# Delta-rule head of a hybrid decoder layer: ScalarE reads, a table load, mask and layer-norm steps put into other slots

## The reference, cut to what matters

```python
proj = rmsnorm(x, g_pre_mix) @ w_in   # q, k, v | beta, decay | z | GLU input | gate a | gate b
qkv  = silu(causal_dwconv(qkv_pre, conv_qkv_w))          # width 4
q, k = l2norm(q) * HEAD_K ** -0.5, l2norm(k)
...
a    = where(strict, beta * (k @ k.T) * exp(gam_i - gam_j), 0)   # chunks of 64 positions
sol  = triangular_solve(a + eye, [beta * v, beta * exp(gam) * k])
...
o    = rmsnorm(o) * silu(z)
glu  = glu_in[..., :CONF_WIDTH] * sigmoid(glu_in[..., CONF_WIDTH:])
c    = causal_dwconv(glu, conf_dw_w) + conf_dw_b         # width 31
o_b  = silu(layernorm(c, conf_ln_g, conf_ln_b))
x    = x + rmsnorm((sigmoid(gate_a) * o + sigmoid(gate_b) * o_b) @ w_out)
y    = x + rmsnorm(square(relu(rmsnorm(x) @ w_up)) @ w_down)
```

## Time and profile before

| | us |
|---|---|
| time, median of 3 runs | 1051.16 (1051.08 to 1052.3) |
| the profiled execution | 1051.12 |
| its span | 1049.3 |
| TensorE busy | 1031.2 (98%), 7929 products |
| VectorE busy | 739.0 (70%) |
| GpSimd busy | 647.9 (62%) |
| ScalarE busy | 595.3 (57%) |
| granted TensorE clock | 0.9 or more of full speed in every slice |

### The profile page before, as it was taken

One profiled execution on the slowest core, in us unless ns is written; L12 is line 12 of the kernel. 1 busy time (PEld: TensorE's weight loads), 2 busy tenths in 40 slices (PEclk: granted clock), 3 DMA queues, 4 the chain that ended last, 5 costly groups with the idle time before them and its releaser, 6 DMA issues.

```text
span 1049.3 us, 21800 instructions
## 1 busy us (share of the span) xinstructions
PE 1031.2 (98%) x7929; PEld 1001.8 (95%) x7929; DVE 739.0 (70%) x1240; ACT 595.3 (57%) x1100; POOL 647.9 (62%) x568
## 2 busy tenths in 40 slices
PE   8999999999999999999999999999999999999997
PEld 6999899999999999999999999999999999999997
DVE  7989898898888988889767757594444444444335
ACT  7865646575565655656747855765444343343632
POOL 1895777785877858677684433647555555555631
PEclk9999999999999999999999999999999999999999
DMA  6322312223132231323221162123322233222302
GB/s 240 114 70 82 108 42 92 95 80 104 43 95 93 96 90 40 94 93 111 96 79 43 54 241 82 41 81 101 101 81 82 81 94 107 80 80 80 119 6 88
DMA packets 33883, 94.36 MB, mean 90 GB/s; under 512 B 4864, under 2 KB 12576, under 8 KB 33824
## 3 DMA queue, kind: packets, MB, share of 16 engines
q1 hardware_dynamic: 33824, 93.57, 27.3%
HBM read 85.02 MB, written 8.53 MB: 89 GB/s over the span
## 4 chain that ended last, share of the span: by engine, by line
PE 81%; DVE 6%; issue 4%; POOL 3%; ACT 3%; DVEq 0%; ACTq 0%; POOLq 0%
PE ps L784 26%; PE ps L1214 15%; PE ps L1162 13%; PE ps L793 7%; PE ps L1246 5%; PE ps L749 3%; DVE ps L1964 2%; DVE t_r L1961 1%; PE ps L936 1%; POOL in_lo L2659 1%; DVE work L2195 1%; PE ps L803 1%; POOL o_a L2659 1%; DVE work L2092 1%; POOL work L2659 1%
## 5 line engine op out<-in xcount | busy, mean ns | idle before, releaser
L2659 POOL TENSOR_TENSOR w_lo<-raw,w_hi 128x1024 fp32r<-128x1024 f32 x100 | 240.8, 2409 | 149.5 <-ACT w_hi L1790 50.2
L784 PE MATMUL ps<-in_hi,w_hi 128*128 128x288 f32 x944 | 285.9, 303 | 1.2 <-ACT work L1447 0.7
L784 PE MATMUL ps<-in_lo,w_hi 128*128 128x288 f32 x944 | 281.8, 300 | 0.7 <-POOL in_lo L2659 0.7
L784 PE MATMUL ps<-in_hi,w_lo 128*128 128x288 f32 x944 | 282.0, 299 | 0.0
L1964 DVE SCALAR_TENSOR_TENSOR ps<-work,ct,ps 128x512 f32<-128x512 f32 x240 | 180.7, 753 | 7.9 <-DVE work L2124 1.6
L784 PEld LDWEIGHTS ps<-in_hi,w_hi 128*128 128x128 f32 x944 | 177.6, 188 | 3.9 <-issue 2.4
L784 PEld LDWEIGHTS ps<-in_hi,w_lo 128*128 128x128 f32 x944 | 177.6, 188 | 0.7 <-issue 0.2
L784 PEld LDWEIGHTS ps<-in_lo,w_hi 128*128 128x128 f32 x944 | 177.2, 188 | 1.0 <-POOL in_lo L2659 0.9
L1961 DVE TENSOR_TENSOR o_a<-o_a,ps 128x576 f32<-128x576 f32 (+1 forms) x63 | 42.8, 682 | 107.6 <-PE ps L1214 73.3
L2659 POOL TENSOR_TENSOR w_lo<-t_pair,w_hi 128x1024 fp32r<-128x1024 f32 x18 | 43.6, 2423 | 42.5 <-ACT w_hi L1819 29.7
L2659 POOL TENSOR_TENSOR work<-work 128x576 f32<-128x576 f32 (+4 forms) x51 | 57.9, 1148 | 15.1 <-PE ps L1049 10.8
(11 more groups left out here) (408 smaller groups left out, 2816.7 us busy)
## 6 DMA issues: line engine op xcount, KB each, us to landing
raw<-w_all_in SPq DMA_DIRECT2D x135, 512.0 KB, 3.7
work<-s_in_in SPq DMA_DIRECT2D x8, 512.0 KB, 3.3
s_sample_out<-work SPq DMA_DIRECT2D x8, 512.0 KB, 4.4
xt<-x_t_in SPq DMA_DIRECT2D x4, 576.0 KB, 6.6
xt<-x_t_in SPq DMA_DIRECT2D x2, 1152.0 KB, 7.2
work<-decay_rows SPq DMA_DIRECT2D x7, 288.0 KB
y_out<-o_a SPq DMA_DIRECT2D x14, 144.0 KB, 1.8
halo<-halos_in SPq DMA_DIRECT2D x9, 156.0 KB, 3.6
```

The costliest lines, as they stand in the source:

```text
L784: t = mm(dense_ps(n, j, h), a[:, w, k], b[:, k, h * HALF:(h + 1) * HALF], start=r == 0, stop=r == PASS_MM // 2 - 1)
L2659: return gp.tensor_tensor(out, a, b, op)
```

## The change

It moves steps between slots. No step of the computation is added or left out but for the pieces into which `um` is cut.

1. TensorE: `MIDDLE_AT` of slots 19 and 20 goes from 11, 8 to 10, 9.
2. ScalarE, passes 1 to 7: the read of CB's first half (slot 18) goes behind the copies to `x_r` and `u_r`; the sigmoid table is loaded in slot 16, behind the casts. In every pass, slot 19 begins with a copy of one quarter of `t_r` into `um`.
3. GpSimd: the rest of `um` is formed in slot 16, after level 6, in two smaller subtractions; `tmi_ready` now counts two a pass.
4. VectorE: the fourth tap of V's convolution goes from slot 19 to slot 20, behind `x_last`; pass 3's table `early_3` changes.
5. Pass 1: the channel sum goes behind `chunk_u` within slot 24.
6. Last pass: the exponentials go from slot 2 to slot 3, with that behind the read of Z's second half and a cast; from slot 17 on layer norm's subtractions and pairs go behind `head(n, s)`; the last pair and the three sums go from slot 19 to slot 20, where they stand behind `x_last`; the squares of slot 18 go behind the `x_r` and `u_r` copies.

```diff
-MIDDLE_AT = (12, 12, 14, 14, 14, 14, 12, 13, 12, 10, 10, 12, 10, 13, 11, 13, 12, 11, 11, 11, 8, 8,
+MIDDLE_AT = (12, 12, 14, 14, 14, 14, 12, 13, 12, 10, 10, 12, 10, 13, 11, 13, 12, 11, 11, 10, 9, 8,
              10, 12, 8, 10, 4, 12, 4, 4, 15, 0)
...
+            def channel_sum(n):
+                act.wait_ge(conv31_done, n)
...
             def phase(n):
-                for s in range(33):
+                def mean_squares(s):
+                    for k in (2 * s - 30, 2 * s - 29):
+                        act.wait_ge(xc_ready, k + 1)
+                        A(xc_squares(k), conf[:, k], ACT.Square).then_inc(xc_sq, 1)
+
+                def read_first(s):
                     pos, j = evac_first(n, s)
...
+                for s in range(33):
+                    if s == 19:
+                        act.wait_ge(t_ready, LEVELS * n)
+                        A(quad(v["um"], 1, 0), quad(t_r, 1, 0).bitcast(F32), ACT.Copy).then_inc(tmi_ready, 1)
+                    if last(n) or s != 18:
+                        read_first(s)
                     pos, j = evac(n, s)
...
                     casts(n, s)
+                    if not last(n) and s == 16:
+                        act.preload_act_table_set("sigmoid_and_others")
...
-                    if s == (11 if last(n) else 24 if n_is(n, 1) else 19):
...
+                    if not n_is(n, 1) and s == (11 if last(n) else 19):
+                        channel_sum(n)
...
-                    if last(n) and 15 <= s < 19:
-
-                        for k in (2 * s - 30, 2 * s - 29):
-                            act.wait_ge(xc_ready, k + 1)
-                            A(xc_squares(k), conf[:, k], ACT.Square).then_inc(xc_sq, 1)
+                    if last(n) and 15 <= s < 18:
+                        mean_squares(s)
...
-                    if s == (3 if n_is(n, 1) else 2):
+                    if s == (3 if n_is(n, 1) or last(n) else 2):
                         act.wait_ge(dm_diff, n)
...
+                    if s == 18 and not last(n):
+                        read_first(s)
+                    if last(n) and s == 18:
+                        mean_squares(s)
                     if s == 22:
...
-                        act.wait_ge(tmi_ready, n)
+                        act.wait_ge(tmi_ready, 2 * n)
...
+                    if n_is(n, 1) and s == 24:
+                        channel_sum(n)
...
                 if s == 20:
 
                     dve.wait_ge(x_ps, LEVELS * n)
-                    dve.wait_ge(tmi_ready, n)
+                    dve.wait_ge(tmi_ready, 2 * n)
                     tt(x_last[:], v["um"][:, 0:SEQ], g(0), ALU.add).then_inc(x_ready, 1)
...
-            early_3 = {1: 4, 2: 1, 3: 2, 8: 2, 12: 1, 14: 1, 16: 1}
+            early_3 = {1: 4, 2: 2, 3: 3, 14: 1, 16: 1, 18: 1}
...
-                halves = (4, 7, 10, 12, 18, 19)
-                if proj and s in halves:
-                    i, half = divmod(halves.index(s), 2)
-                    qkv_conv(n, i, 2 * half, 2 * half + 2)
+                parts = {4: (0, 0, 2), 7: (0, 2, 4), 10: (1, 0, 2), 12: (1, 2, 4), 18: (2, 0, 2), 19: (2, 2, 3), 20: (2, 3, 4)}
+                if proj and s in parts:
+                    qkv_conv(n, *parts[s])
...
+            def layer_norm(s):
+
+                if 14 <= s < 18:
+                    for k in (2 * s - 28, 2 * s - 27):
+                        if k == 0:
+                            dve.wait_ge(mu_ready, 1)
+                        tt(two(conf[:, k]), two(conf[:, k]), job_ps(1), ALU.subtract).then_inc(xc_ready, 1)
+                if s in (16, 17, 18, 20):
+                    k = 6 if s == 20 else 2 * s - 32
+                    dve.wait_ge(xc_sq, k + 2)
+                    tt(xc_squares(k), xc_squares(k), xc_squares(k + 1), ALU.add).then_inc(xc_pair, 1)
...
+                    if last(n) and s < 17:
+                        layer_norm(s)
                     head(n, s)
+                    if last(n) and s >= 17:
+                        layer_norm(s)
...
-                    if last(n) and s == 19:
+                    if last(n) and s == 20:
                         for i, (a, b) in enumerate(((0, 2), (4, 6), (0, 4))):
                             dve.wait_ge(xc_pair, (2, 4, 6)[i])
                             tt(xc_squares(a), xc_squares(a), xc_squares(b), ALU.add).then_inc(xc_pair, 1)
...
+                    if s == 16:
+
+                        pool.wait_ge(t_ready, LEVELS * n - 1)
+                        pool.wait_ge(conv31_s, 2 * n)
+                        for a in range(2):
+                            rows, columns = (slice(0, HP), slice(0, P))[a], slice(a * HP, a * HP + HP)
+                            tt(pr(v["um"])[rows, :, columns], pr(t_r.bitcast(F32))[rows, :, columns],
+                               con("ident")[rows, columns].unsqueeze(1).to_broadcast([HP + a * HP, TILES, HP]), ALU.subtract)
+                        gp.tensor_copy(sample_half(0), by_sample(v["qn"][:, SEQ:TOK])).then_inc(tmi_ready, 1)
...
-                    if s == 19:
-
-                        pool.wait_ge(t_ready, LEVELS * n)
-                        pool.wait_ge(conv31_s, 2 * n)
-                        tt(pr(v["um"]), pr(t_r.bitcast(F32)), bc(con("ident")), ALU.subtract)
-                        gp.tensor_copy(sample_half(0), by_sample(v["qn"][:, SEQ:TOK])).then_inc(tmi_ready, 1)
```

More of the change, by code:

```diff
@@ L1479, in v_tile @@
                 A(v["vts"][0:SMP], g(3)[0:SMP, 0:P], ACT.Copy).then_inc(vt_ready, 1)
+            def channel_sum(n):
+                act.wait_ge(conv31_done, n)
+                dst = conf[:, n - 1] if isinstance(n, int) else \
+                    conf[:, bass.ds(n - 1, 1)].rearrange("p a b -> p (a b)")
+                A(dst[:, 0:SEQ], acc31(), ACT.Identity, bias=ct[:, CF_TAPS:CF_TAPS + 1])
+                A(dst[:, SEQ:TOK], v["c31"][:, SEQ:TOK], ACT.Identity,
+                  bias=ct[:, CF_TAPS:CF_TAPS + 1]).then_inc(conf_ready, 1)
+                if not last(n):
+                    act.wait_ge(conf_ready, n)
+                    act.wait_ge(taps_cur, 2 * n + 1)
+                    A(ct[:], tap_of(n)[:, 3 * QK_TAPS:TAPW], ACT.Copy).then_inc(taps_cur, 1)
             def samples_u(n):
```

## The result

The changed kernel takes 1053.05 us (median; 1051.5 to 1054.34) where the kernel before took 1051.29 beside it: ratio 1.0017, 95% interval 1.001 to 1.0023. It is slower by 1.8 us, 0.17%: by the median just inside the 0.2% that the forecast called no change (the interval reaches 0.23%), but outside the range (1048.0 to 1052.4) and on the other side of the 0.4 us that were expected. The profiled execution took 1053.69, 2.6 more than that of before (1051.12); its span is 1051.9 against 1049.3.

What follows compares the result with a forecast made beforehand. TensorE, busy 98%, bounds the kernel; gains lie in its waits in the eight passes. −0.5 − 0.2 − 0.45 − 0.25 − 1.37 + 2.4 = −0.4 from 1051.1 gives 1050.7 us, range 1048.0 to 1052.4.

Steps and rivals of the forecast that it cites:

- Last pass, slots 20 and 21: Variance product in the last pass waits for square sums now behind `x_last`: +2.4 us, bounds +1.4 to +3.8.
- The place behind `x_last`: On VectorE in the last pass, four adds standing after `x_last` end later: 1.4 us late.
- the split: GpSimd's weight split of slot 20, last pass, may hold VectorE's adds: 1.0 us taken, at worst 2.42, at best 0.
- the middle passes: Passes 3 to 7, slots 16 to 22: earlier `x_r` copy shortens TensorE's wait; −0.5 us, bounds −2.2 to +0.5.
- the tap: V's fourth convolution tap behind `x_last`, passes 3 to 7, delays the subtraction TensorE needs: +0.10 us a pass.
- Slot 17: Last pass: head ahead of layer norm's subtractions on VectorE removes TensorE's wait; −1.37 us, bounds −1.37 to −1.0.
- The read of Z: Last pass, slots 2 and 3: TensorE's wait goes, GpSimd's mask product limits the gain; −0.25 us, bounds −0.83 to 0.
- Pass 3's slot 14: No convolution tap ahead of the `t_r` update on VectorE, so TensorE's wait goes; −0.45 us, bounds −0.45 to 0.
- Passes 1 and 2: Chunk 0's wait goes but the stall moves to GpSimd's state decay; −0.2 us, bounds −1.0 to +0.3.
- Faster: Rival: middle passes pay in full and last-pass adds meet no split; −3.1 us, 1048.0, chance 0.18.
- Slower, by CB's read: Rival: read of CB's first half holds Z's first product, slot 20, seven passes; 2.9 us more, 1053.6, chance 0.09.
- Slower by the table switch: Rival: switch holds ScalarE 1.28 us beyond the load, `uc_r` copy late in seven passes; +9, 1060, chance 0.03.

## Why the prediction was wrong

**The step that failed** is "Last pass, slots 20 and 21": "+2.4 (+1.4 to +3.8)". It measured 4.38. The wait itself was sized almost rightly: 2.75 against 2.4. The place behind `x_last` is worth 1.4, as said (1.42 stays without the split), and the split held the adds 1.27 where 1.0 was taken. What was missing is that a wait on TensorE can cost more than its length: the clock came back at half and that took 1.63 more. No term, bound or rival held this. The three executions in which no fall shows took 1051.5 to 1051.9, inside the range. With the 1.63, the upper bound of the step would have been some 5.4 and the range would have reached 1054. The range was also narrower than its own bounds: the adds at +3.8 and the middle passes at +0.5 give 1050.7 + 1.4 + 1.0 = 1053.1, not 1052.4. That would just have held the measured time, but by luck, since neither bound has the clock in it. The rows read could not show the clock's part: the longest idle time in them is 1.21, with the clock full in its window. But the trace of before had it, in a window that the prediction did not open, the last one of the span, where TensorE has been idle since its last product ended at 1045.6:

```profile
1046.00:1048.00 2.00, 0.00 (x0) 0.00 (x0) 0.00 (x0) 0.02 (x1) 0.00 (x0) 1.00 0.95 334
1048.00:1049.00 1.00, 0.00 (x0) 0.00 (x0) 0.00 (x0) 0.00 (x0) 0.00 (x0) 0.57 0.42 149
```

A forecast of a wait twice as long as that of the earlier trace rows should have sent the reader there.

**The middle passes** were the other miss: −0.5 forecast, +0.02 measured, inside the bounds given. The gain came as worked out (0.25 of 0.27 after what the moved product gives back), the load cost 0.10 for 0.07. The mis-sized term is the tap: 0.20 for 0.10. The prediction costed the tap behind `x_last` but never asked what VectorE would do ahead of it, where an idle time of 0.86 had opened.

**Right, step by step.** Slot 17: −1.40 for −1.37. The read of Z: all of it goes and most comes back at slot 10, −0.16 for −0.25. Pass 3's slot 14: −0.61 for −0.45. Passes 1 and 2: −0.22 for −0.2, but not where it was said, and in part by luck: the shift rises by 0.15 in pass 1, where nothing was forecast, and falls by 0.37 in pass 2, where 0.3 was. The stall of chunk 0 comes back not at the state decay but six microseconds later, at a state update behind five taps on VectorE:

```profile
113.30 0.49 PE L1033 MATMUL ps<-work 128*128 128x128 f32 x2 [0.91 <-DVE work L1983]
```

**The rivals.** Faster: its two conditions were tested one by one. The adds without the split give 1050.03; the passes with the tap moved back give 0.7 to 0.8 in all, where it had 2.2 for the middle passes paying in full. Slower, by CB's read: did not happen, 0.17 us away. Slower by the table switch: the load of 349.69 ends at 350.97 and the copy starts at 350.99. The Trainium skill, "ScalarE: Activation LUTs", section "What ACT_TABLE_LOAD costs", has a drain of some 1380 ns there; the trace shows 0.02 us behind the load and 0.02 ahead of it (the cast before it ends at 349.67), and decides. With the page "SBUF — State Buffer" of the Trainium skill, section "🔬 SBUF: two separate sides", and its exclusive lock of VectorE and GpSimd, the 4.15 and 2.88 above agree.

**Not settled.** The 0.45 at 612 us stands behind a weight block that lands 1.3 us later against TensorE's products. The same stall shows in two other kernels with the 2.7 us wait (0.4 and 0.3), not in the third, nor in the ones without that wait. It looks like a consequence of it, but was not tried by itself. Two corrections to the text ahead of the prediction: VectorE's passes 2 and 3 are written out too, its loop begins at 4; and the pass whose timelines are called pass 4 there, in the expectations and here is the fifth by the bounds of the passes. No number depends on it.

## What to carry to other kernels

A new wait on TensorE is to be priced twice, by its length and by what the clock may do behind it, and where it is longer than any in the trace the range has to say that it doesn't know. When work is moved behind an instruction on its engine, look at both sides of the new place: what now runs beside it on an engine that can hold it, as GpSimd's split held these adds, and the idle time that opened where it left. A wait can be shortened by putting independent products ahead of it, or by making the neighbour start later; here one semaphore wait on GpSimd was worth 2.9 us by the trace.

## What was not expected of the hardware

In a stream at full clock, TensorE's granted clock went to half behind an idle time of 2.69 us (0.64 and 0.51 in the two windows after it) and also behind one of 1.72 (0.55), and stayed full behind 1.62 and 1.42 at the same place, and behind the 1.21 of the earlier trace rows. The length of the wait does not decide alone. All ten traces of this case have an idle time of 1.59 ahead of the first product of L1278 near the end. In eight the clock stays full behind it; in two, of the experiments with the sums alone at slot 19 and with the tap alone moved back, it falls. The window from 1044 us of the first of these:

```profile
1044.00:1046.00 2.00, 2.00 (x6) 1.43 (x5) 1.40 (x4) 0.89 (x3) 1.89 (x3) 0.52 0.00 0
```

From the first product of L1278 to the end of the span these two took 7.99 and 8.01 us, the kernels before and after 6.92 each: 1.1 more. Executions of one kernel differ in the same way: three of the sixteen of the changed kernel show no fall, and so do five of the eleven with the tap moved back, which kept the wait of 2.7 us. What decides besides the length was not tried. With the fall, four products that take 0.81 us took 1.58, and dense products 0.24 instead of 0.133.
